# Output projections of a two-block transformer kernel: from one float32 product to three products of float32r halves

## The reference, cut to what matters

```
x = layer_norm(ALPHA * x + 0.5 * swiglu(x, ...))          # ffn0
y = mixer(x)              # layer 0: mixer_ab (16 heads of 64), layer 1: mixer_c (16 heads of 64)
x = layer_norm(ALPHA * x + y)                             # y ends in  o @ w_out   (1024 x 1024)
y = memory_attn(x, mem)   # 4 heads of 256, y ends in  o @ w_o   (1024 x 1024)
x = layer_norm(ALPHA * x + y)
x = layer_norm(ALPHA * x + 0.5 * swiglu(x, ...))          # ffn1
```

## Time and profile before

| what | value |
|---|---|
| median of 3 runs | 2966.43 us (2966.04 to 2969.21) |
| the profiled execution | 2972.83 us |
| its span in the trace | 2971.0 us |
| TensorE matmul busy | 2758.7 us, 93% of the span |
| VectorE busy | 1584.7 us, 53% |
| ScalarE busy | 1100.0 us, 37% |
| mean granted TensorE clock | 0.972 of full speed |

### The profile page before, as it was taken

How to read it: one execution, slowest core, us unless ns; L and a number is a source line. 1 busy time by engine, 2 the same in 40 slices (tenths; PEclk the granted TensorE clock), 3 DMA queues, 4 the chain that set the end, 5 groups by cost and what they waited for, 6 DMA issues and landing times.

```text
span 2971.0 us, 35644 instructions
## 1 busy us (share of the span) xinstructions
PE 2758.7 (93%) x15307; PEld 2120.9 (71%) x15307; DVE 1584.7 (53%) x1694; ACT 1100.0 (37%) x1272; POOL 140.8 (5%) x117
## 2 busy tenths in 40 slices
PE   8999989999999999988779999998799899999998
PEld 6786676887878677877456468875464588888887
DVE  3455535455455435456663354465743447566687
ACT  3432433434344334333310144333201245455475
POOL 0002000000021000001011000010110000000000
PEclk9999999999999999999989999999799899999999
DMA  6554234556553335544322445553214157565696
GB/s 250 207 184 142 71 128 159 186 193 208 179 175 114 133 123 184 198 147 163 115 69 71 146 140 185 178 174 111 92 58 143 54 193 250 188 226 205 217 319 238
DMA packets 226570, 484.09 MB, mean 163 GB/s; under 512 B 11535, under 2 KB 44943, under 8 KB 225967
## 3 DMA queue, kind: packets, MB, share of 16 engines
q1 hardware_dynamic: 226032, 478.16, 47.6%
q10 hardware_dynamic: 380, 3.66, 0.5%
HBM read 477.07 MB, written 2.95 MB: 162 GB/s over the span
## 4 chain that ended last, share of the span: by engine, by line
PE 80%; DVE 12%; ACT 3%; DMA 2%; issue 2%; POOL 1%; SPq 0%; ACTq 0%; DVEq 0%; POOLq 0%
PE psum L408 18%; PE psum L410 18%; PE psum L409 18%; PE psum L411 14%; PE psum L2149 2%; DVE weight_ring_low_halves L403 2%; PE psum L529 1%; PE psum L2901 1%; PE psum L2235 1%; DVE stage_area_halves L520 1%; PE psum L909 1%; ACT weight_high_halves L397 1%; DMA weight_ring<-in_ffn_w_gate 1%; PE psum L621 1%; DVE small L961 1%
## 5 line engine op out<-in xcount | busy, mean ns | idle before, releaser
L403 DVE TENSOR_TENSOR weight_ring_low_halves<-weight_ring,weight_high_halves 128x2048 fp32r<-128x2048 f32 (+2 forms) x336 | 737.4, 2208 | 648.3 <-ACT weight_high_halves L397 648.0
L408 PE MATMUL psum<-weight_high_halves,stage_area_halves 128*128 128x512 f32 (+2 forms) x2522 | 969.4, 384 | 65.0 <-DVE stage_area_halves L520 46.2
L410 PE MATMUL psum<-weight_high_halves,stage_area_halves 128*128 128x512 f32 (+2 forms) x2522 | 959.9, 381 | 0.0
L409 PE MATMUL psum<-weight_ring_low_halves,stage_area_halves 128*128 128x512 f32 (+4 forms) x2316 | 881.4, 381 | 0.0
L397 ACT ACTIVATE weight_high_halves<-weight_ring 128x2048 fp32r<-128x2048 f32 (+2 forms) x336 | 617.3, 1849 | 594.4 <-PE psum L410 301.0
L408 PEld LDWEIGHTS psum<-weight_high_halves,stage_area_halves 128*128 128x128 f32 x2522 | 478.8, 190 | 166.1 <-DVE stage_area_halves L520 39.5
L410 PEld LDWEIGHTS psum<-weight_high_halves,stage_area_halves 128*128 128x128 f32 x2522 | 478.4, 190 | 95.1
L409 PEld LDWEIGHTS psum<-weight_ring_low_halves,stage_area_halves 128*128 128x128 f32 x2316 | 439.5, 190 | 83.6
L411 PE MATMUL psum<-weight_ring,stage_area 128*128 128x512 f32 x1088 | 480.1, 601 | 5.8 <-issue 5.8
L411 PEld LDWEIGHTS psum<-weight_ring,stage_area 128*128 128x128 f32 x1088 | 207.7, 193 | 263.7 <-issue 263.4
L510 ACT ACTIVATE stage_area<-psum 128x512 f32<-128x512 f32 (+3 forms) x134 | 74.3, 561 | 497.5 <-PE psum L410 200.8
(11 more groups left out here) (288 smaller groups left out, 2124.3 us busy)
## 6 DMA issues: line engine op xcount, KB each, us to landing
weight_ring<-in_ffn_w_gate SPq DMA_DIRECT2D x44, 1024.0 KB, 5.2
weight_ring<-in_ffn_w_up SPq DMA_DIRECT2D x44, 1024.0 KB, 5.2
weight_ring<-in_ffn_w_down SPq DMA_DIRECT2D x44, 1024.0 KB, 5.1
weight_ring<-in_w_in SPq DMA_DIRECT2D x36, 1024.0 KB, 5.1
weight_ring<-in_moe_wd SPq DMA_DIRECT2D x30, 1024.0 KB, 5.0
weight_ring<-in_moe_wg SPq DMA_DIRECT2D x23, 1024.0 KB, 5.5
weight_ring<-in_moe_wu SPq DMA_DIRECT2D x23, 1024.0 KB, 6.8
weight_ring<-in_mem_w_kv SPq DMA_DIRECT2D x16, 1024.0 KB, 5.1
```

Of the source, the lines that this page charges most:

```text
L403: v.raw.tensor_tensor(self.low_half(name), self.in_slot(name), self.high_half(name), ALU.subtract).then_inc(*v.mark("low_halves", ("halves ...
L408: pe.raw.matmul(out, a[1], w[0], start=start, stop=False)
L409: pe.raw.matmul(out, a[0], w[1], start=False, stop=False)
L410: return pe.raw.matmul(out, a[0], w[0], start=False, stop=stop)
```

## The change

The four output projections are planned with `split=True`, and the attentions take their result out of PSUM as halves, high at column 10240 and low at column 2048 of the stage area. The splits of the new pieces are placed in the attentions' loops: in the mixers one piece at the end of each of the steps 1, 3, 5 and 7 (`out_cuts`), on ScalarE behind `turned` and on VectorE behind `normalise`; in the memory attention two pieces before the loop and one each at the end of the steps 1 and 2. `out(g)` now exists on ScalarE too, behind `turned`, and VectorE's `out(g)` waits for it. The second block's attention keeps the old form (`halves=False`).

```diff
+        self.oT_halves = (self.halves_part(10240, KT, S), self.halves_part(2048, KT, S))
...
@@ attn_vector
+def attn_vector(net, v, tag, heads, per_group, cuts=None):
...
     def out(g):
         v.wait_ge(*v.at((tag, "values", g)))
         src = net.ps[:, 4 + g % 2, :].rearrange("p (a t) -> p a t", a=2)
+        if cuts is not None:
+            net.halves_copy(v, tuple(t[:, 2 * g:2 * g + 2, :] for t in net.oT_halves), src, 4 + g % 2, (tag, "values", g), (tag, "oT", g))
+            return
...
             out((i - 3) // per_group)
+        if cuts is not None:
+            net.split_vector(v, cuts.get(i, []))
@@ attn_scalar
+    def out(g):
+        src = net.ps[:, 4 + g % 2, :].rearrange("p (a t) -> p a t", a=2)
+        net.halves_copy(act, tuple(t[:, 2 * g:2 * g + 2, :] for t in net.oT_halves), src, 4 + g % 2, (tag, "values", g), (tag, "oT", g))
 
-    for i in range(n + 1):
+    for i in range(n + 1 if cuts is None else n + 3):
         if i < n:
             exps(i)
-        if i >= 1:
+        if 1 <= i <= n:
             turned(i - 1)
+        if cuts is not None:
+            if i >= 3:
+                out(i - 3)
+            net.split_scalar(act, cuts.get(i, []))
@@ pairs_vector
+        if to["halves"]:
+            net.halves_copy(v, tuple(t[:, 2 * g:2 * g + 2, :] for t in net.oT_halves), src, 6 + g % 2, (tag, "values", g), (tag, "oT", g))
+            return
         v.raw.tensor_copy(net.oT[:, 2 * g:2 * g + 2, :], src).then_inc(*net.drained(v, 6 + g % 2, (tag, "values", g), (tag, "oT", g)))
 
     for p in range(n + 3):
...
         if p >= 3 and (p - 3) % 2 == 1:
             out((p - 3) // 2)
+        net.split_vector(v, cuts.get(p, []))
@@ pairs_scalar
+    def out(g):
+        src = net.ps[:, 6 + g % 2, :].rearrange("p (a t) -> p a t", a=2)
+        net.halves_copy(act, tuple(t[:, 2 * g:2 * g + 2, :] for t in net.oT_halves), src, 6 + g % 2, (tag, "values", g), (tag, "oT", g))
+
+    for p in range(n + 3):
         if p < n:
             exps(p)
-        if p >= 1:
+        if 1 <= p <= n:
             turned(p - 1)
+        if to["halves"] and p >= 3 and (p - 3) % 2 == 1:
+            out((p - 3) // 2)
+        net.split_scalar(act, cuts.get(p, []))
@@ First
+                st["mix_out"] = net.plan_proj("ab_out", ins["ab_w_out"][0], blocks(D), KT, split=True)
...
+                st["mix_out"] = net.plan_proj("c_out", ins["c_w_out"][0], blocks(D), KT, split=True)
...
+            st["mo"] = net.plan_proj(f"mem{i}_o", ins["mem_w_o"][i], blocks(D), KT, split=True)
...
+    def out_cuts(self, st):
+        return {2 * j + 1: [piece] for j, piece in enumerate(st["mix_out"]["pieces"])}
+
     def tensor(self, pe):
         net = self.net
-        oT = lambda k, m: net.oT[:, k, m * P:(m + 1) * P]
+        oT = lambda k, m: pick(net.oT_halves, k, m)
@@ First.scalar
+                pairs_scalar(net, act, "ab", self.ab_heads(), self.ab_pairs, self.out_cuts(st))
...
-            net.projT_copy(act, st["mq"], range(4), net.qT, ["scalar"])
-            attn_scalar(net, act, f"mem{i}", self.mem_heads(i))
+            net.projT_copy(act, st["mq"], range(4), net.qT, ["scalar"], [0, 1])
+            net.split_scalar(act, st["mo"]["pieces"][:2])
+            net.projT_copy(act, st["mq"], range(4), net.qT, ["scalar"], [2, 3])
+            attn_scalar(net, act, f"mem{i}", self.mem_heads(i), {p: [st["mo"]["pieces"][p + 1]] for p in (1, 2)})
@@ First.vector
+                pairs_vector(net, v, "ab", self.ab_heads(), self.ab_pairs, self.out_cuts(st))
...
-            attn_vector(net, v, f"mem{i}", self.mem_heads(i), 1)
+            net.split_vector(v, st["mo"]["pieces"][:2])
+            attn_vector(net, v, f"mem{i}", self.mem_heads(i), 1, {p: [st["mo"]["pieces"][p + 1]] for p in (1, 2)})
```

More of the change, by code:

```diff
@@ L786, in attn_tensor @@
             values(i - 2)
-def attn_vector(net, v, tag, heads, per_group, need_bias=()):
+def attn_vector(net, v, tag, heads, per_group, cuts=None):
     n = len(heads)
@@ L842, in attn_vector, with attn_scalar @@
             out((i - 3) // per_group)
-def attn_scalar(net, act, tag, heads):
+        if cuts is not None:
+            net.split_vector(v, cuts.get(i, []))
+def attn_scalar(net, act, tag, heads, cuts=None):
     n = len(heads)
@@ L939, in pairs_tensor, with pairs_vector @@
             values(p - 2)
-def pairs_vector(net, v, tag, heads, to):
+def pairs_vector(net, v, tag, heads, to, cuts={}):
     n = len(heads) // 2
@@ L997, in pairs_vector, with pairs_scalar @@
             out((p - 3) // 2)
-def pairs_scalar(net, act, tag, heads, to):
+        net.split_vector(v, cuts.get(p, []))
+def pairs_scalar(net, act, tag, heads, to, cuts={}):
     n = len(heads) // 2
@@ L1034, in turned @@
             act.raw.activation(to["pT"][:, j], src, ACT.Copy).then_inc(*net.drained(act, 4 + j, (tag, "turned", p, j), (tag, "pT", p, j)))
-    for p in range(n + 1):
+    def out(g):
+        src = net.ps[:, 6 + g % 2, :].rearrange("p (a t) -> p a t", a=2)
+        net.halves_copy(act, tuple(t[:, 2 * g:2 * g + 2, :] for t in net.oT_halves), src, 6 + g % 2, (tag, "values", g), (tag, "oT", g))
+    for p in range(n + 3):
         if p < n:
             exps(p)
-        if p >= 1:
+        if 1 <= p <= n:
             turned(p - 1)
+        if to["halves"] and p >= 3 and (p - 3) % 2 == 1:
+            out((p - 3) // 2)
+        net.split_scalar(act, cuts.get(p, []))
 def head(q, k, v, out, scale, nk=1, bias=None, sink=None, need=()):
@@ L1150, in __init__ @@
         biased = [net.pair_part(16384 + 1024 * u) for u in range(2)]
-        self.ab_pairs = dict(probs=[net.pair_part(8192), net.pair_part(9216)], pT=net.pair_part(12288),
+        self.ab_pairs = dict(halves=True, probs=[net.pair_part(8192), net.pair_part(9216)], pT=net.pair_part(12288),
                              inverse=net.part(18432, 2 * MT, P), biased=lambda p: biased[p % 2],
                              sinks=lambda p: self.sink[:, 2 * p - 8:2 * p - 6])
-        self.c_pairs = dict(probs=[net.pair_part(8192), net.pair_part(9216)], pT=net.pair_part(0),
+        self.c_pairs = dict(halves=True, probs=[net.pair_part(8192), net.pair_part(9216)], pT=net.pair_part(0),
                             inverse=net.part(1024, 2 * MT, P), biased=lambda p: self.bias[p % 3])
@@ L1179, in __init__ @@
                 st["mv"] = net.plan_proj("mem0_v", ins["mem_w_kv"][0][:, D:2 * D], blocks(D), KT)
-                st["mix_out"] = net.plan_proj("ab_out", ins["ab_w_out"][0], blocks(D), KT)
+                st["mix_out"] = net.plan_proj("ab_out", ins["ab_w_out"][0], blocks(D), KT, split=True)
             else:
@@ L1185, in __init__ @@
                 st["c_k"] = net.plan_proj("c_k", w[:, D:2 * D], blocks(D), KT, split=True)
-                st["mix_out"] = net.plan_proj("c_out", ins["c_w_out"][0], blocks(D), KT)
+                st["mix_out"] = net.plan_proj("c_out", ins["c_w_out"][0], blocks(D), KT, split=True)
             wkv = ins["mem_w_kv"][i]
@@ L1192, in __init__ @@
             st["mq"] = net.plan_proj(f"mem{i}_q", ins["mem_w_q"][i], blocks(D), KT, split=True)
-            st["mo"] = net.plan_proj(f"mem{i}_o", ins["mem_w_o"][i], blocks(D), KT)
+            st["mo"] = net.plan_proj(f"mem{i}_o", ins["mem_w_o"][i], blocks(D), KT, split=True)
             self.load_norm(4 * i + 3)
@@ L1412, in scalar @@
                 net.turn_copy(act, self.ab_turn())
-                pairs_scalar(net, act, "ab", self.ab_heads(), self.ab_pairs)
+                pairs_scalar(net, act, "ab", self.ab_heads(), self.ab_pairs, self.out_cuts(st))
             else:
@@ L1422, in scalar @@
                 net.projT_copy(act, st["c_k"], range(4), net.kT, ["scalar"])
-                pairs_scalar(net, act, "c", self.c_heads(), self.c_pairs)
+                pairs_scalar(net, act, "c", self.c_heads(), self.c_pairs, self.out_cuts(st))
             act.wait_ge(*act.at((("ab", "c")[i], "oT", 3), *[("memT", m, kg) for m in range(MT) for kg in (0, 4)]))
@@ L1512, in vector @@
                 net.turn_copy(v, self.ab_turn())
-                pairs_vector(net, v, "ab", self.ab_heads(), self.ab_pairs)
+                pairs_vector(net, v, "ab", self.ab_heads(), self.ab_pairs, self.out_cuts(st))
             else:
                 net.split_vector(v, st["c_q"]["pieces"] + st["c_k"]["pieces"])
-                pairs_vector(net, v, "c", self.c_heads(), self.c_pairs)
+                pairs_vector(net, v, "c", self.c_heads(), self.c_pairs, self.out_cuts(st))
             v.wait_ge(*v.at(("mem_high", i)))
@@ L1614, in __init__ @@
         biased = [spare[:, 1024 * u:1024 * u + 1024].rearrange("p (j m k) -> p j m k", j=2, m=MT) for u in range(2)]
-        self.dsa_pairs = dict(probs=[net.pair_part(8192), net.pair_part(9216)], pT=net.pair_part(12288),
+        self.dsa_pairs = dict(halves=False, probs=[net.pair_part(8192), net.pair_part(9216)], pT=net.pair_part(12288),
                               inverse=spare[:, 2048:2560].rearrange("p (i t) -> p i t", t=P), biased=lambda p: biased[p % 2])
```

## The result

| | median | runs | profiled execution | its span | granted clock |
|---|---|---|---|---|---|
| before | 2966.43 us | 3 (2966.04 to 2969.21) | 2972.83 us | 2971.0 us | 0.972 |
| after | 3076.54 us | 3 (3074.72 to 3079.93) | 3074.72 us | 3072.9 us | 0.957 |

The ratio on record is 1.0363, with a 95% interval of 1.0339 to 1.0388 (the two medians alone give 1.0371): slower by 110 us between the medians, and by 102 between the two profiled executions. The forecast was 3074.

A forecast was written before the change was run, and what follows sets the result against it. Projections were taken as bound by TensorE, mixers' attentions by no full engine but by hand-overs. -20.0 + 76.1 + 23.8 + 28 = +107.9 on the median 2966.4 gave 3074 us; range 3043 to 3103.

The forecast's parts named there:

- The mixers' rounds: In the attentions of `ab` and `c`, steps with a split or `out` become serial across engines: +76.1 us at full clock.
- The memory attentions: In both memory attentions, split waits at steps 1 and 2 delay the turnings: +11.9 us each, +23.8 together.
- the walk: Attention steps laid end to end in queue order at full clock: 81.4 us for `ab`, 81.6 for `c`.
- The products: In the four output projections, 96 half products replace 32 float32 ones each: 112.4 to 92.4 us, a gain of 20.0.
- cold start: Each mixer's projection follows an idle TensorE and so takes 1.6 us more.
- The clock: TensorE's gaps between rounds lower its clock: 2.0 us for each of 13 mixer gaps, 1 per memory attention, +28 us.
- no clock cost: Rival: scores and values break TensorE's gaps, so it stays at the high clock level; 3046 us, chance 0.18.
- low throughout: Rival: TensorE's low clock level never lifts in the mixers' attentions, 50 us instead of 26; 3098 us, chance 0.12.
- Behind the projections: `mk`'s last piece lands 0.7 us later, its layer norm waits, but VectorE's 6.94 us of idle time absorbs it: nothing.
- The sum: Whole kernel: all terms together add 107.9 us to the time before, giving 3074 us; chance 0.58.
- Busy time alone: Rival: VectorE pays only for its added work, with ScalarE's high halves ready when asked: +9, 2975 us, chance 0.06.
- all hidden: Rival: splits fit VectorE's idle time in the mixers' attentions, so only the products count: 2946 us, chance 0.04.

The follow-up runs named there:

- VectorE two steps late: Changed kernel with VectorE's low halves and half copies two steps later in the mixers' loops, same instructions; 2985.07 us.
- the waits alone: Kernel before the change, with only waits for ScalarE's turned(p-1) added on VectorE at the end of the mixers' steps 1 and 3 to 8; 3036.06 us.
- all mended: Changed kernel with splits outside all four attentions' loops and VectorE's half copies one step later; 2956.41 us, ratio 0.9945 to the kernel before.
- the gaps filled: Changed kernel plus five unused 128x512 matmuls on TensorE ahead of the turnings 1 and 3 to 7 of each mixer; 3058.11 us.
- `out` alone late: Changed kernel with VectorE's half copies in the mixers one step later, splits left in place; 3047.78 us.
- the memory as before: Changed kernel with both memory outputs put back to float32 products without halves or splits, mixers still changed; 3063.57 us.
- the memory mended: Changed kernel with only the memory attentions edited: last two pieces split behind the loop, VectorE's half copies one step later; 3056.25 us.

## Why the prediction was right, point by point

- **The mixers' rounds.** Walked 81.4 and 81.6 us at full clock (`ab`, `c`), with 12 and 14 of clock 93.4 and 95.6. Measured 93.28 and 93.45: `ab` as walked, `c` 2.2 us less. Shown by the ring of waits above, by VectorE two steps late (the same work, 46.6 us), and from the other end by the waits alone.
- **The memory attentions.** In the walk the second and third turnings end 13.4 and 20.4 us behind the first scores (432.7 and 439.7 less 419.29). In the chain of the kernel after, with its start at 467.75, the turnings end at 481.19 and 488.16, 13.4 and 20.4:

```profile
478.94 0.61 DVE small L809
...
480.52 0.67 PE psum L759 x4
...
481.71 1.91 ACT weight_high_halves L398
483.64 2.29 DVE weight_ring_low_halves L404
...
487.50 0.66 PE psum L759 x4
488.16 3.42 PE psum L774 x8
```

  The stretches grew by 12.6 and 13.9, where I had 11.9 and 1 of clock: +26.5 against 25.8.
- **The products.** 0.232 us each, as `c_v` has them. Here a term was mis-sized: I added 1.6 us for each mixer's projection as a cold start (first matmuls at the low clock). Neither had one: 22.24 and 22.45 at a mean clock of 1.00, behind only 1.5 us of idle time. The gain was 23.0, not 20.0. A cold start did come in `ab` in two other versions: 23.57 at 0.94 with all mended, and this with the gaps filled, where a product's matmuls still come 0.43 us apart 3 us into it:

```profile
373.44:398.50 25.06, 25.05 (x97) 20.18 (x97) 7.44 (x4) 7.61 (x4) 0.00 (x0) 0.88 0.30 97
```

  And it came in `c` in three: 23.6 with `out` alone late, 23.8 with the memory as before, 24.0 with the memory mended. An idle TensorE earlier on doesn't tell which; see the last section. By the Trainium skill's rule of four passes for a true float32 product ("FP8 and Floating Point Precision", "TensorE Precision Notes") an estimate is three quarters of 27.70, 20.8; these traces have 22.3, four fifths.
- **The clock.** Taken: 12 us in `ab`. In the kernel after, the turnings there take 26.8 us, at 393 ns, and the values 11.8, at 505. With all mended, which has the clock of before, they are 16.4 and 8.7:

```profile
L924 PE MATMUL psum<-stage_area 128*128 128x128 f32 x128 | 16.4, 281 | 3.4 <-DVE stage_area L999 3.1
L940 PE MATMUL psum<-stage_area 128*64 128x256 f32 x64 | 8.7, 391 | 1.3 <-ACT stage_area L1054 1.3
```

  That is 13.5 more on TensorE, nearly all of it in the ring. The rivals "no clock cost" (3046) and "low throughout" (3098) both fall: a turning of `ab` behind 5.5 to 8.3 us of idle time takes 3.75 to 3.78 us, the one at 315.13 that follows other matmuls takes 2.05. The gaps were as many as the walk had: six cold turnings in `ab` and seven in `c`, of 3.40 to 3.78 us. In step 5 the price on the path was 2.6 and not 2.0, but over all it was 2.0: turnings and values take 38.6 and 37.8 us in the two mixers, where full clock makes 16.4 + 8.7 each, 26.2 more for 13 gaps. And filling the gaps, which brought most of the clock back, shortened the attentions by as much as it shortened these matmuls. The Trainium skill's "TensorE: Matmul & The Clock Gate", section "HAM oscillation", describes bursts between waits for DMA that each start throttled. Here the waits are for another engine; the trace agrees with its pattern for the turnings, and the 2.9 us a gap that the prediction estimated by it is too much.
- **Behind the projections.** VectorE's slack behind the norm beside `mk` shrank from 6.94 to 6.39, 0.55 where I had 0.7, and nothing came of it:

```profile
434.45 4.49 DVE L404 TENSOR_TENSOR weight_ring_low_halves<-weight_ring,weight_high_halves 128x2048 fp32r<-128x2048 f32 x2 [6.39 <-ACT weight_high_halves L398]
```

- **The sum.** +107.9 was predicted against the profiled execution, which the stretches put at +103.3 and the two executions at +101.9: 3 us less for the projections, 2 less for `c` (95.6 walked with its clock, 93.45 in the trace). The medians differ by 110.1, because the profiled execution of before stood 6.4 us above its median and that of after 1.8 below. So the closeness of 3074 to 3076.5 is part luck; the terms were each off by up to 3 us. Two slips in the working change nothing: the terms of `ab`'s round add up to 12.9 and not 12.8, and the upper end of the range by its own bounds, 3098 + 3, is 3101 and not 3103.
- **The other rivals.** "Busy time alone" (2975) and "all hidden" (2946) are not what this order gives. "All hidden" describes the version with all mended well: 2956 measured, and 2950 by its ratio on 2966. The gain was in the change all along; the order gave it away.

What stays open: the clock's exact part in the 110 us. TensorE's turnings and values are 26.2 us longer in the two mixers than at full clock, and filling the gaps gave back 20.1 us there. That the remaining 6 would come back one for one is argued, not shown, and the clock's part in the memory attentions, taken as 1 us each, is not parted: with the same instructions these take 29.8 us at a mean clock of 0.89 and 31.2 at 0.84.

## What to carry to other kernels

When two engines share a piece of work, place each half by what it hangs on. A consumer's wait must not stand in its queue right behind the instruction that starts the chain it waits for, with the next round's first work behind it. That turned a software pipeline into one serial ring and doubled the stage: 93.3 us against 46.6 for the same instructions with VectorE's half two steps later. Two steps of lag gave back 90% of what `ab` had lost, and places outside the loops with `out` one step late all but 0.5 us (41.8 against 41.3). To price such a change, don't add up busy times: walk one step in order of the queues, and add the granted clock of an engine that now stands still in between.

## What was not expected of the hardware

- The gap just ahead of a turning doesn't tell its speed. With the waits alone, where gaps come at each step, turnings take 3.58 us behind 1.89 us of idle time, 3.68 behind 2.33 and 3.65 behind 4.17, and the mean clock of the stage is 0.81. In the kernel before a turning behind 2.04 us takes 2.05, and the one slow turning stands behind 4.36 us. `ab`'s first turning comes behind the scores of one pair and, ahead of these, a gap of 2.79 us in four versions alike: it takes 2.05 us in the kernels before and after, 3.68 with the waits alone and 3.44 with VectorE two steps late. What decides it stays open; so a price for the clock taken from the long gaps alone was too low by 11 us or more in the waits alone.
- Useless work can pay. Thirty products of 128x512 in each mixer's attention, which nothing uses, made the kernel 18 us faster, in a single run that the stretches bear out (20.1 us less in the two attentions). The turnings of `ab` alone fell from 26.8 us to 19.4.
- Whether a projection starts cold is not told by the stage in front of it. In the kernel after, the stage's mean clock is 0.74, the last turning is cold (3.78 us, at 378.02), then come gaps of 1.28 and 1.53 us, and the projection starts at full clock. With all mended the mean is 0.99, the last turning takes 2.02, the same two gaps follow, and the projection starts low. TensorE's timeline of that one, with its first matmuls, which in the kernel after take 0.39 to 0.47:

```profile
331.03 1.08 PE L940 MATMUL psum<-stage_area 128*64 128x256 f32 x8 [1.28 <-ACT stage_area L1054]
333.64 0.77 PE L409 MATMUL psum<-weight_high_halves,stage_area_halves 128*128 128x512 f32 x1 [1.53 <-issue]
334.20 0.63 PE L410 MATMUL psum<-weight_ring_low_halves,stage_area_halves 128*128 128x512 f32 x1
```

  What decides it stays open; it is worth 1 to 3 us a time.
